# First recurrence of a two-layer block: its row of decays read from a DRAM scratch, output banks returned one by one, output weights grouped by order of use

## What is computed

```python
def _even_layer(x, segs, C0, n0, m0, h0, conv0, pre_g, post_g, w_in, w_out, ...):
    hn = _rmsnorm(x, pre_g)
    q, k, v, og, ig, fg, z, xr, gr = _split(einsum('bld,de->ble', hn, w_in))
    ... per segment: _mlstm_segment(q, k, v, log_i, log_f, C, n, m)   # chunks, decay weights, states
    hm = _head_norm(sigmoid(og) * hm, m_norm_g) * silu(z)
    hl = _rglru(...) * silu(gr)
    out = einsum('ble,ed->bld', concat([hm, hl]), w_out)
    return x + _rmsnorm(out, post_g), states
```

## Time and profile before

| | us |
|---|---|
| median of 3 runs (2212.53 to 2216.96) | 2212.78 |
| the profiled execution's own time | 2214.64 |
| span of its trace | 2212.9 |
| TensorE matmul busy | 2069.8 (94%) |
| DVE busy | 1324.6 (60%) |
| ACT busy | 844.9 (38%) |
| POOL busy | 273.2 (12%) |
| mean granted TensorE clock | 0.97 |

### The profile page before, as it was taken

One profiled execution on the slowest core, in us unless ns is written; L12 is line 12 of the kernel. 1 busy time (PEld: TensorE's weight loads), 2 busy tenths in 40 slices (PEclk: granted clock), 3 DMA queues, 4 the chain that ended last, 5 costly groups with the idle time before them and its releaser, 6 DMA issues. The chain is left out here.

```text
span 2212.9 us, 32966 instructions
## 1 busy us (share of the span) xinstructions
PE 2069.8 (94%) x12662; PEld 1851.1 (84%) x12662; DVE 1324.6 (60%) x2299; ACT 844.9 (38%) x1536; POOL 273.2 (12%) x384
## 2 busy tenths in 40 slices
PE   5999999999998799999958999999999699999998
PEld 4999999999998577787737999999999476767774
DVE  5456676645655666766646656655666575555653
ACT  5455543322322444343445444222222353333433
POOL 3000000000000111111121000000000242323222
PEclk8999999999999799999979999999999799999999
DMA  2111233343232544454331332443233544545442
GB/s 100 56 63 62 63 111 88 126 146 118 85 111 81 210 134 136 134 158 143 97 125 44 101 95 78 134 148 127 90 107 99 177 168 144 170 148 178 169 148 69
DMA packets 204480, 262.26 MB, mean 119 GB/s; under 512 B 47585, under 2 KB 151265, under 8 KB 202289
## 3 DMA queue, kind: packets, MB, share of 16 engines
q1 hardware_dynamic: 204336, 260.30, 36.7%
HBM read 170.29 MB, written 89.97 MB: 118 GB/s over the span
## 5 line engine op out<-in xcount | busy, mean ns | idle before, releaser
L547 DVE TENSOR_TENSOR pa_stage<-pa_ps,pa_stage 128x536 f32<-128x536 f32 x110 | 77.1, 713 | 129.4 <-PE pa_ps L514 121.4
L547 DVE TENSOR_TENSOR pc_stage<-pc_ps,pc_stage 128x536 f32<-128x536 f32 x110 | 77.1, 713 | 104.8 <-PE pc_ps L514 91.7
L362 PE MATMUL pa_ps<-a_XT_hi,pa_w_hi 128*128 128x358 f32 x576 | 133.1, 339 | 0.3 <-PEq L197 0.3
L362 PE MATMUL pa_ps<-a_XT_hi,pa_w_lo 128*128 128x358 f32 x576 | 126.0, 327 | 0.0
L362 PE MATMUL pa_ps<-a_XT_lo,pa_w_hi 128*128 128x358 f32 x576 | 125.7, 326 | 0.0
L1407 PE MATMUL ma_ps<-ma_wout_hi,ma_mix_hi 128*128 128x512 f32 x256 | 106.2, 415 | 6.9 <-DVE ma_residual L1441 6.9
L514 PE MATMUL pc_ps<-c_XT_hi,pc_w_lo 128*128 128x268 f32 x384 | 110.2, 287 | 0.0
L514 PE MATMUL pc_ps<-c_XT_hi,pc_w_hi 128*128 128x268 f32 x384 | 110.2, 287 | 0.0
L514 PE MATMUL pa_ps<-a_XT_hi,pa_w_lo 128*128 128x268 f32 x384 | 110.1, 287 | 0.0
L514 PE MATMUL pc_ps<-c_XT_lo,pc_w_hi 128*128 128x268 f32 x384 | 110.1, 287 | 0.0
L514 PE MATMUL pa_ps<-a_XT_lo,pa_w_hi 128*128 128x268 f32 x384 | 110.1, 287 | 0.0
(11 more groups left out here) (544 smaller groups left out, 6172.6 us busy)
## 6 DMA issues: line engine op xcount, KB each, us to landing
pa_w_raw<-in_w_a SPq DMA_DIRECT2D x57, 512.0 KB, 4.6
pc_w_raw<-in_w_c SPq DMA_DIRECT2D x49, 512.0 KB, 4.7
scr_c<-pc_stage SPq DMA_DIRECT2D x48, 512.0 KB, 3.2
scr_a<-pa_stage SPq DMA_DIRECT2D x40, 512.0 KB, 3.2
ma_hin<-scr_a SPq DMA_DIRECT2D x32, 512.0 KB, 3.7
mc_hin<-scr_c SPq DMA_DIRECT2D x32, 512.0 KB, 3.7
mc_sample_state<-in_s SPq DMA_DIRECT2D x32, 512.0 KB, 4.6
out_s_s<-mc_sample_state SPq DMA_DIRECT2D x32, 512.0 KB, 2.9
```

The lines of the kernel that those rows point to most:

```text
L362: ins = pe.matmul(self.ps[:, 3 * s + t, 0:TC], w[:, k, :], x[:, k, t * TC:(t + 1) * TC], start=(k == 0 and j == 0), stop=(k == KT - 1 and ...
L547: dve.tensor_tensor(dst, self.out(p, product), x, ALU.add).then_inc(self.added, 1)
```

## The change

It does seven things. (1) The rows `S.rrow` are stored to a new DRAM scratch `scr_r` in the projection of A; in mix A each step loads its 128 numbers to all partitions (`row`, two buffers, 64 KB), on the same semaphore as `hin`; L1717 is gone and L1967 reads `row`. (2) In both mixes the norm of a block handles one output bank after the other (scale, add, give back). (3) TensorE does both weight tiles of a half on bank 6 first, then both on bank 7, and waits for each bank singly. (4) Layer A's weights are split into early and late by order of use. (5) In mix A `acc` is doubled and DVE's `sample_num` goes behind the unit's read and update. (6) In mix C the squares of `norm_samples` go to `gn` in SBUF, and TensorE waits for `os_sum` in place of `sqs_chain`. (7) ACT's `norm_samples` goes behind `part_m`.

```diff
@@ stage_project_a, SP
                 sp.dma_start(out_m, m_out[:]).then_inc(finished, 16)
+                sp.dma_start(row_d, S.rrow[:]).then_inc(finished, 16)
@@ OutWeights.load
-                     self.w_d[:, bass.ds(self.first + 2 * pair, 2), :]).then_inc(...)
+                     self.w_d[:, bass.ds(self.list[2 * pair], 2), :]).then_inc(...)
@@ OutRing
-    def products(self, pe, ps, n, i, e, first, last, new_w):
+    def products(self, pe, ps, n, tiles, freed, new_w):
         if new_w:
-            pe.wait_ge(self.w_ready, self.order.index(e) + 1)
+            pe.wait_ge(self.w_ready, max(self.order.index(e) for i, e in tiles) + 1)
         for half in range(2):
             cols = slice(half * 512, half * 512 + 512)
+            if freed:
+                pe.wait_ge(self.out_read, freed - 1 + half)
+            for i, e in tiles:
...
         dve.wait_ge(self.y_stored, 16)
-        for half in range(2):
-            dve.scalar_tensor_tensor(out=ps[:, 6 + half, :], ...).then_inc(self.scaled, 1)
         dve.wait_ge(self.x_in, 16 * c + 16)
         for half in range(2):
             cols = slice(half * 512, half * 512 + 512)
+            dve.scalar_tensor_tensor(out=ps[:, 6 + half, :], ...).then_inc(self.scaled, 1)
             dve.wait_ge(self.scaled, 2 * c + half + 1)
             ins = dve.tensor_tensor(self.yx[:, cols], ps[:, 6 + half, :], self.yx[:, cols], ALU.add)
@@ stage_mix_a
+OUT_ORDER_A = [8, 9, 0, 1, 10, 11, 2, 3, 12, 13, 4, 5, 14, 15, 6, 7]
+        row = [a.sb(f"ma_row{s}", [P, P]) for s in range(2)]
-        acc = a.sb("ma_sample_inter", [2 * NS, MV])
+        acc = [a.sb(f"ma_sample_inter{s}", [2 * NS, MV]) for s in range(2)]
                     sp.dma_start(hin[n % 2][:, :, 0:rows], scr_d[c, h, :, 0:8, 0:rows]).then_inc(hin_in[n % 2], 16)
+                    sp.dma_start(row[n % 2][0:rows, 0:rows], row_d[h:h + 1, c * P:c * P + rows].to_broadcast([rows, rows])
+                                 ).then_inc(hin_in[n % 2], 16)
-                    pe.wait_ge(hin_in[n % 2], 16 * (n // 2) + 16)
+                    pe.wait_ge(hin_in[n % 2], 32 * (n // 2) + 32)
-                    pe.matmul(ps[0:rows, 0, 128:128 + rows], S.sel[:, h, 0:rows], S.rrow[:, c * P:c * P + rows], ...)
-                    dve.scalar_tensor_tensor(out=ei[0:rows, 0:rows], in0=ps[0:rows, 0, 128:128 + rows],
+                    dve.scalar_tensor_tensor(out=ei[0:rows, 0:rows], in0=row[n % 2][0:rows, 0:rows],
@@ mix A, DVE, step n
-                    if n in aux_of and aux_of[n][0] == "own":
-                        sample_num(aux_of[n][1])
                     if u is not None:
                         read_sample(u)
                         update_sample(u)
+                    if n in aux_of and aux_of[n][0] == "own":
+                        sample_num(aux_of[n][1])
@@ stage_mix_c, PE unit
-                            pe.wait_ge(sqs_chain, 3 * g - 2)
+                            pe.wait_ge(os_sum, g)
@@ stage_mix_c, ACT
-                    root_of_mean(sqs_chain, 4, NS, gns[:], ps[0:NS, 2, :], g)
+                    root_of_mean(sqs_chain, 4, NS, gns[:], gn[0:NS, :], g)
...
-                    u = unit_of(n - 1)
-                    if u is not None and u % NSEQ == NSEQ - 1:
-                        norm_samples(u // NSEQ)
                     if h == 0 and c:
                         act.wait_ge(c_done, n + 1)
                         O.post_act(act, ps, c - 1, gn[:])
                     part_m(n)
+                    u = unit_of(n - 1)
+                    if u is not None and u % NSEQ == NSEQ - 1:
+                        act.wait_ge(c_done, n + 1)
+                        norm_samples(u // NSEQ)
@@ build_program
-            w_early = OutWeights(S, make_alloc(nc, raw_rows), "wout_a_early", io["w_oa"], 8, 8)
+            w_early = OutWeights(S, make_alloc(nc, raw_rows), "wout_a_early", io["w_oa"], OUT_ORDER_A[0:8])
-            w_late = OutWeights(S, make_alloc(nc, raw_rows), "wout_a_late", io["w_oa"], 0, 8)
+            w_late = OutWeights(S, make_alloc(nc, raw_rows), "wout_a_late", io["w_oa"], OUT_ORDER_A[8:16])
```

More of the change, by code:

```diff
@@ L1197, with __init__ @@
 class OutWeights:
-    def __init__(self, S, a, name, w_d, first, tiles):
+    def __init__(self, S, a, name, w_d, list):
+        tiles = len(list)
         self.rows = a.sb(name, [P, tiles, D])
-        self.w_d, self.first, self.tiles = w_d, first, tiles
+        self.w_d, self.list, self.tiles = w_d, list, tiles
         self.loaded = S.a.sem(f"{name}_in")
@@ L1206, in load @@
         sp.dma_start(self.rows[:, bass.ds(2 * pair, 2), :],
-                     self.w_d[:, bass.ds(self.first + 2 * pair, 2), :]).then_inc(self.loaded if done is None else done, 16)
+                     self.w_d[:, bass.ds(self.list[2 * pair], 2), :]).then_inc(self.loaded if done is None else done, 16)
 class OutProjection:
@@ L1249, in w_lo @@
     def w_lo(self, e):
-        return self.w_low[:, (e - self.early.first) % 16, :]
+        return self.w_low[:, (self.early.list + self.late.list).index(e), :]
     def raw(self, e):
-        w = self.early if self.early.first <= e < self.early.first + self.early.tiles else self.late
-        return w.rows[:, e - w.first, :]
+        w = self.early if e in self.early.list else self.late
+        return w.rows[:, w.list.index(e), :]
     def split_w_hi(self, act, k):
         for e in self.order[4 * k:4 * k + 4]:
-            if self.late and self.late.first <= e < self.late.first + self.late.tiles:
-                act.wait_ge(self.late_in[(e - self.late.first) // 2], 16)
+            if e in self.late.list:
+                act.wait_ge(self.late_in[self.late.list.index(e) // 2], 16)
             else:
@@ L3163, in build_program @@
             raw_rows = ExitStack()
[L3164 removed]
+            w_early = OutWeights(S, make_alloc(nc, raw_rows), "wout_c_early", io["w_oc"], list(range(10)))
             with ExitStack() as xctx:
```

63 lines of the change are left out of this document (27 added, 36 removed).

## The result

The changed kernel takes **2183.48 us** (median of 4 runs, 2182.56 to 2187.39) against 2214.04 in the runs of the kernel before beside them: ratio 0.9862, 95% interval 0.9849 to 0.9874, 30.6 us. The prediction was 2185.7 us, range 2179 to 2197. The two profiled executions stand 27.25 us apart (2214.64 and 2187.39); the other 3.3 us come from the choice of executions: the profiled one of after was the slowest of its four, at a mean granted clock of 0.968 where the other three had 0.970.

A forecast was written before the change was run, and what follows sets the result against it. TensorE, busy 94% of the span, was taken as the bound in the mixes. Terms 12.4 + 0.4 + 3.3 + 1.8 + 0.9 + 7.1 + 1.2 = 27.1 us, from the median of 2212.78 to 2185.7 us; range 2179 to 2197.

The forecast's parts named there:

- Selector matmul: Mix A, 20 full-size ordinary steps: removing L1717 shortens each by 0.62 us, 12.4 us in all.
- Banks, post steps: Mix A, n = 5, 13, 21, 29: output starts 1.2 us earlier, but the update waits for state_ready; 0.1 each, 0.4 us.
- Own steps: Mix A, n = 9, 17, 25: sample_num behind the update gains 0.85 to 1.45 us, taken as 1.1 each, 3.3 us.
- Last block: End of mix A: three narrow selector matmuls at 0.2 us each, full bank gain of 1.1 at n = 33; 1.8 us together.
- Start: Mix A's steps 0 to 3: DVE gets scores sooner, though the first row may land 0.5 us behind hin; 0.9 us.
- Weights: Mix A's start: storing the weights by order of use brings nothing, as no wait for a weight load shows.
- Added DMAs: Mix A: 36 row loads and one store on SP cost nothing, landing in 2.8 us under 9.4 us of cover.
- Shared ports: Rival, mix A: POOL holds L1967 for 0.6 us in each of 32 steps, 19 us lost, 2204.9 us; chance 0.03.
- Mix C: Waits of 3.57 us at n = 9 and 17 vanish, 7.1 us; banks given back singly add 1.2 us.
- DVE does not take back half: Rival, mix A: DVE's chain halves the ordinary steps' gain; post, own and start give nothing; 2196.5 us, chance 0.12.
- `norm_samples` costs nothing: Mix C: the move behind part_m costs nothing; the rival has ACT late three times by 1.7 us, 2190.8 us, chance 0.07.
- the row is late once: Rival, mix A: row landing later than 9.4 us delays steps; at 12 us it loses 83 us, 2269 us; chance 0.04.

The follow-up runs named there:

- x1_row: Kernel before with the row loaded by DMA and no selector matmul, nothing else: 2199.12 us, ratio 0.9922.
- y4_row_first: Changed kernel with each head's row load issued ahead of its hin load: 2185.18 us, ratio 0.9872 to the kernel before.
- x3_banks: Kernel before with the output banks handled and given back one by one in both mixes, nothing else: 2213.25 us, ratio 0.9992.
- y5_banks_together: Changed kernel with the two output banks given back together again, as before the change: 2186.22 us, ratio 0.9877 to the kernel before.
- x4_num: Kernel before with acc doubled and DVE's sample_num behind the unit's read and update, nothing else: 2209.21 us, ratio 0.9972.
- y6_weights: Changed kernel with layer A's weights stored early and late as before the change: 2185.65 us, ratio 0.9864 to the kernel before.
- x2_mixc: Kernel before with only mix C's two norm edits: squares to SBUF with the wait on os_sum, norm_samples behind part_m. 2204.56 us, ratio 0.9947.
- x5b_osum: Kernel before with norm_samples' squares in their own bf16 SBUF tile and TensorE waiting on os_sum, norm_samples still ahead of part_m: 2203.06 us, ratio 0.9944.
- z1: Changed kernel plus: weight splitting behind part_m, row load first, state update ahead of divide in seven post steps, sample_num's division behind part_m. 2176.87 us, ratio 0.9837.
- y2_split_m: Changed kernel with DVE's weight splitting in steps 0 to 3 moved behind part_m: 2181.68 us, ratio 0.9856 to the kernel before.

## Why the prediction was right, and where it was off

The total came out 2.2 us from the measured median. Most of the mechanisms were right; that the sum is so close is in part luck, because its terms err in both directions (mix C 3.4 us too little, the start 2.6 too much) and 1.7 us between the mixes were lost that no edit touches.

*Selector matmul:* 0.62 forecast, 0.60 measured, in 20 steps when the clock doesn't fall at n = 4 (9.78 us in x1_row, 9.79 in y4_row_first, from 10.39). Right, and for the reason given: x1_row.

*Banks, post steps:* 0.4 forecast, -0.22 measured, the mechanism right (x3_banks, y5_banks_together). L1797 started at R + 8.44, where R + 8.42 was forecast, by two errors that cancel: the state update ended at R + 8.39 and not R + 8.28 (DVE's list grew by 0.26 us, not 0.15), and TensorE followed 0.06 us behind it and not 0.14. What I left out is the longer first pair of matmuls behind idle time.

*Own steps:* 3.3 forecast, 4.38 measured; 4.6 in x4_num. The size that failed is "then follows at once ... 0.85 us" and the middle of 1.1 taken from it. The high end, 1.45, was right: L2079 no longer runs beside POOL and takes 0.42 us, so `mp_ready` is only just in time, and the wait forecast in front of L1752 does not come up.

*Last block:* 1.8 against 1.88. That is luck. The narrow selector matmuls are four, not three (72 rows of L1717, 8 of them 16 columns wide), and gave 0.13 and 0.14 where they can be seen, not 0.2. n = 33 gave 2.03 us and n = 34 took 0.42 back. Of the 2.03 most is clock: x4_num has the same wait of 1.17 us at n = 33 and its step took 9.71 us, before 11.02. Timeline of PE at the end of that gap, and the clock in the 4 us there, before, then x4_num:

```profile
1108.41 0.74 PE L1410 MATMUL ma_ps<-ma_wout_hi,ma_mix_hi 128*112 128x512 f32 x1 [1.17 <-DVE ma_residual L1441]
1108.40:1112.40 4.00, 3.99 (x11) 2.51 (x12) 3.03 (x12) 2.02 (x8) 0.30 (x1) 0.64 0.51 198
```

```profile
1103.37 0.46 PE L1410 MATMUL ma_ps<-ma_wout_hi,ma_mix_hi 128*112 128x512 f32 x1 [1.17 <-DVE ma_residual L1441]
1103.37:1107.37 4.00, 4.00 (x16) 2.56 (x17) 3.76 (x14) 2.02 (x8) 0.31 (x1) 1.00 0.51 197
```

So at the full clock the banks and one narrow matmul are worth 0.72 us of the step (9.71 to 8.99) and 0.4 together with n = 34, under the 1.1 of the forecast, and 1.31 us are the slow stretch behind the gap. In x1_row eight matmuls ran at least 0.43 us apart there, and the step took 12.34 us.

*Start:* 0.9 forecast, 1.5 with n = 4 as an ordinary step, and 1.14 lost in this profile. The row lands last, as I wrote, but it puts off the first transposes by 1.4 us, not 0.5. To n = 3 the start gained 1.16 us all the same. Then n = 4 took 12.69 us where it was 10.39: the clock fell behind 3.48 us of idle time. Busy time and clock, after, then y4_row_first:

```profile
782.00:786.00 4.00, 4.00 (x12) 3.16 (x12) 0.90 (x2) 1.05 (x3) 0.73 (x1) 0.50 0.52 124
```

```profile
784.00:788.00 4.00, 4.00 (x24) 3.45 (x23) 3.48 (x11) 1.69 (x7) 0.23 (x1) 1.00 0.73 157
```

With the row, first issue to n = 4 takes 73.6 to 73.9 us (x1_row, y4_row_first, y5_banks_together) or 75.9 to 76.1 (after, y6_weights); without it 74.95 to 74.99 (before, x3_banks, x4_num) or 75.7 to 76.2 (x2_mixc, x5b_osum). So the change is worth 1.1 to 1.4 us of the 1.5 between undisturbed profiles and nothing between disturbed ones; that the stretch misses by 2.6 us is mostly the clock at n = 4, which fell in the profile of after and not in that of before.

*Weights:* nothing, and nothing (y6_weights). *Added DMAs:* no wait in any step but the first. *Shared ports:* L1969 has the durations of L1967. The Trainium skill, SBUF — State Buffer, section "SBUF: two separate sides", says that a DVE instruction with two SBUF inputs and a GpSimd instruction that reads SBUF lock each other out. The add of `sample_num` agrees with it: 0.99 us where it starts just behind POOL's instruction, 0.42 where it starts ahead of it (x3_banks) or after its end (x4_num, after). For L1969 no run here shows it: in none of its 36 steps does a POOL instruction run beside it.

*Mix C:* 7.1 forecast for the two gaps, 10.7 measured (x2_mixc, x5b_osum). The step that failed is "That is 3.57 us at n = 9 and n = 17": a gap was priced by its idle time, and the clock behind it was not read, though the rows were in the trace. `norm_samples` behind `part_m` costs nothing, as forecast. Banks: 1.2 forecast, 0.8 in the eight post steps of this profile, where n = 13 lost 0.30 that it didn't lose in z1.

*The rivals:* DVE does not take back half (x1_row: the full 0.61 in ordinary steps), `norm_samples` costs nothing, the row is late once, and the ports cost nothing because L1969 and POOL never meet here.

Left open: what sets whether a gap of a given length drops the clock. Its length alone does not: step n = 34 of mix C has the same gap of 0.28 us at its head in after and in y2_split_m and took 9.39 and 10.97 us, with seven output matmuls 0.43 us apart in the second. The 1.73 us lost ahead of mix C's n = 4 aren't the change's either: from the last `part_c` of mix A to the first transposes of mix C, the profiles take 603.8 to 607.4 us, and from there to n = 0 15.1 to 16.8, in both kinds of kernel. Nor are the 0.90 us ahead of mix A: the first issue there stands at 714.8 to 717.9 us in the kernels whose projection of A is that of before.

## What to carry to other kernels

A gap of TensorE costs its idle time and, in some executions, a slow stretch behind it (0.2 to 3.0 us behind 3.57, nothing or 1.3 behind 1.17); read the clock and the spacing of the matmuls behind each gap before you price its removal, and look at the same gap in a second profile. When a wait is taken away ahead of an engine that feeds on another's list, find the next semaphore from that same list: the banks came 1.1 us sooner and the state did not, and only the last block and mix C kept the gain. Price a moved instruction by the neighbours it will have, not by those it had.

## What the runs showed of the hardware

- The same idle gap of 3.57 us cost 3.75, 5.35 and 6.54 us in profiles of identical code, by the granted clock behind it (1.00, 0.63 and 0.50 in 4 us). Undisturbed steps agree to 0.02 us, so I put most of the spread between runs (2211.94 to 2219.08 us for the kernel before) down to such places; that was not tried by itself.
- A 64 KB load that spreads one row over 128 partitions takes 4.1 us to land, longer than the 3.4 us of a 512 KB head issued ahead of it, and delays that head to 5.1 us if issued first.
- The first pair of matmuls behind 0.9 us of idle time (L1797) lasts 0.50 to 0.51 us in place of 0.41, in all seven post steps of mix A with a unit, at a granted clock of 1.00.
- A DVE add with two SBUF inputs took 0.97 to 1.00 us where it started 0.01 to 0.04 us behind a POOL instruction (the first three own steps of the kernel before, x1_row, x2_mixc and x5b_osum) and 0.41 to 0.42 us in every other place.
